# A decoder block on eight cores: sigmoids and the softmax division on ScalarE, another order for the output projection, and a prologue in 256-token pieces

## The reference, cut to what matters

```python
u = _rmsnorm(h, norm1_w[l])
proj = u @ w_in[l]                                    # (B,T,D_IN)
aq, ak, av, gq, gk, gv, g_lr, g_r, gate_a, gate_b = jnp.split(proj, offs, axis=-1)
attn_o = _swa_sink_attention(aq, ak, av, attn_sinks[l])   # window 128, softmax with one sink logit per head
gate_logit = (g_lr @ gla_gate_w2[l] + gla_gate_b[l]).astype(jnp.float32)
log_a = jax.nn.log_sigmoid(gate_logit) / GLA_GATE_NORMALIZER
gla_o = _gla(gq, gk, gv, log_a)                       # gated linear attention, 4 heads, state 256x512
gla_o = _rmsnorm(gla_o, gla_norm_w[l])                # per head
gla_o = gla_o * jax.nn.silu(g_r)
merged = jax.nn.sigmoid(gate_a) * attn_o + jax.nn.sigmoid(gate_b) * gla_o
h = h + merged @ w_out[l]
v2 = _rmsnorm(h, norm2_w[l])
h = h + (jax.nn.silu(v2 @ w_ffn_gate[l]) * (v2 @ w_ffn_up[l])) @ w_ffn_down[l]
return _rmsnorm(h, final_norm_w)
```

## Time and profile before

| | us |
|---|---|
| Three timed runs | 4012.56, 4039.02, 4191.10 (median 4039.02) |
| The profiled execution, its own time | 3989.18 |
| Its span, slowest core (core 5) | 3987.6 |
| Spans of all cores | 3979.7 to 3987.6 |
| Mean granted TensorE clock | 0.978 to 0.979 on all cores |
| TensorE busy (matmuls) | 3767.8 (94%) |
| VectorE busy | 1285.7 (32%) |
| ScalarE busy | 806.1 (20%) |
| Reciprocals on VectorE, 64 of 128x512 in the attention | 214.5 |
| ACT_TABLE_LOAD, 20 of them | 25.7 |

### The profile page before, as it was taken

One profiled execution on the slowest core, in us unless ns is written; L12 is line 12 of the kernel. 1 busy time (PEld: TensorE's weight loads), 2 busy tenths in 40 slices (PEclk: granted clock), 3 DMA queues, 4 the chain that ended last, 5 costly groups with the idle time before them and its releaser, 6 DMA issues.

```text
span 3987.6 us, 46220 instructions; the slowest of 8 cores (3979.7 to 3987.6 us)
## 1 busy us (share of the span) xinstructions
PE 3767.8 (94%) x18016; PEld 1700.6 (43%) x18016; DVE 1285.7 (32%) x2070; ACT 806.1 (20%) x1549; POOL 194.3 (5%) x361
## 2 busy tenths in 40 slices
PE   4899999996899999999999999999869999999998
PEld 1444444442344444444454444444324444444443
DVE  1225555556331110011112464646553111110113
ACT  1223232322221110000012232323313000000002
POOL 0000000000000000000000000000000000000000
PEclk9999999998999999999999999999989999999999
DMA  6234343435365555457863434333256555555553
GB/s 152 45 64 69 64 69 64 69 64 119 67 166 119 111 102 85 71 109 146 161 126 64 69 64 69 64 69 64 43 137 153 106 109 119 119 106 93 134 103 111
DMA packets 81416, 382.75 MB, mean 96 GB/s; under 512 B 9264, under 2 KB 10416, under 8 KB 44592
## 3 DMA queue, kind: packets, MB, share of 16 engines
q0 software_dynamic: 36432, 260.19, 39.2%
q1 hardware_dynamic: 44768, 119.59, 9.2%
HBM read 594.84 MB, written 44.04 MB: 160 GB/s over the span
## 4 chain that ended last, share of the span: by engine, by line
PE 91%; DVE 4%; DMA 2%; issue 1%; ACT 1%; POOL 0%; DVEq 0%; SPq 0%; ACTq 0%; POOLq 0%
PE ps L331 89%; DMA px_231<-xT 1%; DVE a_t_93 L378 1%; PE ps L339 1%; PE ps L619 1%; DMA h_0_96<-x 1%; DVE xnT_102 L375 1%; POOL st L399 0%; DVE xn_100 L375 0%; DVE mT L369 0%; ACT g_Sb L355 0%; DVE xn_101 L375 0%; DVE g_U L375 0%; DVE a_t_94 L364 0%; DVE a_t_93 L364 0%
## 5 line engine op out<-in xcount | busy, mean ns | idle before, releaser
L378 DVE RECIPROCAL a_t_93<-a_t_93 128x512 f32<-128x512 f32 x64 | 214.5, 3352 | 6.6
L355 ACT ACTIVATE sg_212<-ps 128x512 bf16<-128x512 f32 x88 | 52.5, 597 | 541.5 <-PE ps L331 541.5
L355 ACT ACTIVATE sg_213<-ps 128x512 bf16<-128x512 f32 x88 | 52.6, 598 | 527.8 <-PE ps L331 527.8
L331 PE MATMUL ps<-v2T_163,wu_67 128*128 128x512 bf16 x576 | 136.1, 379 | 0.0
L331 PE MATMUL ps<-v2T_108,wu_68 128*128 128x512 bf16 x576 | 136.1, 379 | 0.0
L331 PE MATMUL ps<-v2T_108,wu_65 128*128 128x512 bf16 x576 | 136.1, 379 | 0.0
L331 PE MATMUL ps<-v2T_108,wu_66 128*128 128x512 bf16 x576 | 136.1, 379 | 0.0
L331 PE MATMUL ps<-v2T_163,wu_69 128*128 128x512 bf16 x576 | 136.1, 379 | 0.0
L331 PE MATMUL ps<-v2T_108,wu_69 128*128 128x512 bf16 x576 | 136.1, 379 | 0.0
L331 PE MATMUL ps<-v2T_163,wu_66 128*128 128x512 bf16 x576 | 136.1, 379 | 0.0
L331 PE MATMUL ps<-v2T_163,wu_65 128*128 128x512 bf16 x576 | 136.1, 379 | 0.0
(11 more groups left out here) (1319 smaller groups left out, 6541.1 us busy)
## 6 DMA issues: line engine op xcount, KB each, us to landing
wu_66<-wmix POOLq DMA_DIRECT2D x24, 1024.0 KB, 13.1
wu_67<-wmix POOLq DMA_DIRECT2D x24, 1024.0 KB, 13.5
wu_65<-wmix POOLq DMA_DIRECT2D x23, 1024.0 KB, 14.4
wu_68<-wmix POOLq DMA_DIRECT2D x23, 1024.0 KB, 11.4
wu_69<-wmix POOLq DMA_DIRECT2D x22, 1024.0 KB, 14.1
wu_69<-wffn POOLq DMA_DIRECT2D x18, 1024.0 KB, 13.4
wu_65<-wffn POOLq DMA_DIRECT2D x18, 1024.0 KB, 14.1
wu_66<-wffn POOLq DMA_DIRECT2D x18, 1024.0 KB, 13.6
```

Of the source, the lines that this page charges most:

```text
L331: r = e.matmul(o_, lhsT=l_, rhs=r_, start=s0, stop=s1)
L355: S.op("act", lambda e: e.activation(out=o_, in_=i_, func=func, scale=scale, **kw), outs, ins)
L378: S.op("dve", lambda e: e.reciprocal(out=o_, in_=a), [o_], [a])
```

## The change

Five things are changed.

1. **Sigmoids.** The two token-major gates (g_r, gate_b) used one Tanh on ScalarE and one VectorE operation each. Now `sigm` makes three ScalarE operations (Exp, Ln, Exp), and VectorE does one product; the second sigmoid is written as bfloat16 (`ttb`). gate_a used Tanh and a VectorE operation; now ScalarE writes exp(-gate_a) straight to its place, and the rest of the sigmoid is part of the division below.
2. **Division.** In `a_back` the denominator is multiplied by 1 + exp(-gate_a) on VectorE, and its inverse is taken by Ln and Exp on ScalarE instead of by the VectorE reciprocal. The separate product with the gate falls away.
3. **End of a head.** `g_chain` yields once more, ahead of the last `s3`, and `weave` no longer runs the overlay to its end. What is left of it is put in front of the next overlay (`chain2`), which gets 18 steps instead of 16.
4. **Order of w_out.** `d_groups` goes through column groups 0 and 1 with the first four tiles, then with the last four, then through groups 2 and 3; one step of the attention rest follows each of the first tiles, where two did.
5. **Prologue.** x comes as four pieces of 256 tokens (`xq`, 2 MB in four transfers each), in twelve buffers. The pieces and the weights are issued on the POOL queue. A sixth weight buffer (printed as `wu_247`) exists for the first pass. Squares are added up on VectorE, so that the sum over inputs is four float32 matmuls per piece; Ln and Exp take the place of square root and reciprocal. The keys and values of the pieces, and the first head's values (`gv`), are computed between the norms. Most constants are set after the second piece.

```diff
+    wu.append(place("wu%d" % NW, [128, 8, 512], BF16, rE))
...
-    free_units = list(range(NW))
+    free_units = list(range(NW + 1))
...
-    def pump():
-        while free_units and wst["next"] < len(plan):
+    def pump(n=999):
+        while n > 0 and free_units and wst["next"] < len(plan):
+            n -= 1
             i = wst["next"]
             wst["next"] += 1
             u = free_units.pop(0)
             where[i] = u
             src, n = plan[i]
...
     def drop(units):
-        free_units.extend(units)
+        free_units.extend(u for u in units if u < NW)
         pump()
...
+    def first_norm_load(p):
+        for kg in range(4):
+            i = (p * 4 + kg) % 12
+            o_, src = px[i][:, :, :].rearrange("p a b -> p (a b)"), xq[p, kg]
+            S.op("pool", lambda e, o_=o_, src=src: e.dma_start(out=o_, in_=src), [o_], [], dma="px%d" % i)
+
+    def first_norm(p):
+        for kg in range(4):
+            sq = psq[kg % 2] if kg else pacc
+            act(sq[:], px[(p * 4 + kg) % 12][:], AF.Square)
+            if kg:
+                vtt(pacc[:], pacc[:], sq[:], ALU.add)
+        b = nps()
+        mm([(b[:, 0:256], onesf[:], pacc[:, q, :], q == 0, q == 3) for q in range(4)])
+        r = prs[p % 2]
+        act(r[:], b[:, 0:256], AF.Ln, scale=1.0 / D, bias=epst[:, 0:1])
+        act(r[:], r[:], AF.Exp, scale=-0.5)
         for k in range(16):
...
+            stt(xin[0][:, k, p * 256:(p + 1) * 256], px[(p * 4 + k // 4) % 12][:, k % 4, :], n1c[:, k:k + 1], r[:],
+                ALU.mult, ALU.mult)
...
+    def sigm(o_, t, p):
+
+        act(t, p, AF.Exp, scale=-1.0)
+        act(t, t, AF.Ln, bias=1.0)
+        act(o_, t, AF.Exp, scale=-1.0)
...
-            act(t[:], b[:, :], AF.Tanh, scale=0.5)
-            stt(rs[:, i, :], t[:], 1.0, b[:, :], ALU.add, ALU.mult)
+            sigm(t[:], t[:], b[:, :])
+            vtt(rs[:, i, :], t[:], b[:, :], ALU.mult)
...
-                act(t[:], b[:, :], AF.Tanh, scale=0.5)
-                vts(ag[:, pr, hf * 512:(hf + 1) * 512], t[:], 0.5, 0.5, ALU.mult, ALU.add)
+                act(ag[:, pr, hf * 512:(hf + 1) * 512], b[:, :], AF.Exp, scale=-1.0)
...
-        recip(t1[:], t1[:])
-        vtt(t2[:], bo[:, :], t1[:], ALU.mult)
-        vtt(v4(t3[:, :]), v4(t2[:, :]), ag[:, :, n * 128:(n + 1) * 128], ALU.mult)
+
+        stt(v4(t1[:, :]), ag[:, :, n * 128:(n + 1) * 128], 1.0, v4(t1[:, :]), ALU.add, ALU.mult)
+        act(t1[:], t1[:], AF.Ln)
+        act(t2[:], t1[:], AF.Exp, scale=-1.0)
+        vtt(t3[:], bo[:, :], t2[:], ALU.mult)
...
             store(sd[h], U[:, :, :].rearrange("p a b -> p (a b)"), "us", ("sd", h))
+        yield
         s3(NT - 1)
         yield
...
-        for _ in overlay:
-            pass
-
...
+        for g, ts in ((0, range(half)), (1, range(half)), (0, range(half, NT)), (1, range(half, NT)),
+                      (2, range(NT)), (3, range(NT))):
...
     first_norm_load(0)
-    pump()
+    pump(2)
+    S.op("pool", lambda e: e.dma_start(out=wg[:, :, :].rearrange("p a b -> p (a b)"), in_=wglr), [wg[:]], [], dma="c5")
+    first_norm_load(1)
+    pump(2)
+    first_norm_load(2)
...
             first_norm(0)
+            first_norm_load(3)
+            pump()
+            kv(0)
             first_norm(1)
+            kv(1)
+            constants()
+            gv(0)
+            gv(1)
+            first_norm(2)
+            gv(2)
+            gv(3)
+            kv(2)
+            first_norm(3)
+            gv(4)
+            gv(5)
+            kv(3)
+            drop(ukv)
+            gv(6)
+            gv(7)
+            drop(uv)
...
-                weave(g_proj(c, h), prev, 32, 16)
+                weave(g_proj(c, h), prev, 32, 18)
...
-                prev = a_chain(c, h, range(NT))
+                prev = chain2(ov, a_chain(c, h, range(NT)))
...
-        for i in range(8):
+        for i in range(12):
             next(dg)
             next(ac, None)
-            if i > 0:
-                next(ac, None)
```

More of the change, by code:

```diff
@@ L274, in build_nc @@
     tts = [G["tt0"], G["tt1"]]
+    ttb = [place("ttb%d" % i, [128, 512], BF16, S.base[tts[i].name][0]) for i in range(2)]
     e8, _ = seq(rE, [("a_P%d" % i, [128, 512], BF16) for i in range(4)] + [("a_t1", [128, 512], F32),
@@ new lines, in build_nc, with constants @@
+    vset(epst[:], EPS)
+    def constants():
+        stg = place("cstage", [128, 4, 128], F32, rXV[1] + 24576 + 4096)
+        load(stg[:], cst, "c1")
+        load(w2[:], w2r, "c4")
+        vcopy(identf[:], stg[:, 0, :])
+        vcopy(identb[:], stg[:, 0, :])
+        vcopy(trilb[:], stg[:, 1, :])
+        vcopy(amask[:], stg[:, 2:4, :])
+        vset(smask[:], 1.0)
+        vset(smask[:, :].rearrange("p (a b) -> p a b", b=128)[:, :, 0:1], 0.0)
+        vset(onesb[:], 1.0)
+        vset(mhalf[:], -0.5)
+        vset(declast[:], 0.0)
+        act(sinkc, sinkc, AF.Exp)
+        vts(negb, negb, -1.0, None, ALU.mult)
@@ L770, in d_groups @@
         h1 = h1lo + h1hi[c]
-        for g in range(4):
-            units = take(2)
-            for t in range(NT):
+        held = {}
+        half = NT // 2
+        for g, ts in ((0, range(half)), (1, range(half)), (0, range(half, NT)), (1, range(half, NT)),
+                      (2, range(NT)), (3, range(NT))):
+            if g not in held:
+                held[g] = take(2)
+            units = held[g]
+            for t in ts:
                 b = nps()
@@ L786, in d_groups @@
                 yield
-            drop(units)
+            if ts[-1] == NT - 1:
+                drop(units)
     def e_groups(c):
@@ L1064, in make_in_maps @@
     cst[:, 3] = j <= i
-    smk = np.ones((128, 512), np.float32)
-    smk[:, 0::128] = 0.0
     shared = {
```

118 lines of the change are left out of this document (50 added, 68 removed).

## The result

The changed kernel takes 3872.86 us (median; 4052.74 before), 0.958 of the kernel before with an interval of 0.946 to 0.970: faster. Its profiled execution took 3860.02 us against 3989.18, 129 us less where the sum had 141. In a second series the median was 3887.58 us, ratio 0.958 [0.952, 0.964].

What follows compares the result with a forecast made beforehand. TensorE, busy 3767.8 of 3987.6 us, was taken as the bound, leaving its stops and cold clock to win. 41 + 32 + 2 x (6 + 28) = 141 off 3989.18 gave 3848 profiled, 3884 timed; range 3830 to 3950.

Steps and rivals of the forecast that it cites:

- Prologue, 41: Start of kernel: first head's values end at 131 instead of 172.1 us, gain 41 us, bounds 22 to 46.
- pieces and weights in turn: Rival, prologue: alternating issue puts piece 1 at 30 and the values' end at 109, gain 63 us; under 1%.
- End of a head, 32: Heads 0 to 2, both chunks: six stops and the cold matmuls behind them vanish, gain 32 us.
- The wait on `g_gn_83` in the middle of a head stays: Middle of a head: TensorE's wait on this linear-attention buffer was claimed to remain, so no gain there.
- Head 3, 6 per chunk: Head 3: three stops per chunk, 1.2 us shorter each, and about 1.6 at the end; 6 us with the clock.
- Start of w_out, 28 per chunk: First w_out tiles beside attention blocks: nine tiles take 45 to 46 us instead of 75.3, gain taken as 28.
- Woven heads, nothing: Woven heads: TensorE stays busy 108 of 108 us, so sigmoids and division change nothing; ScalarE rises to 65.5.
- Table loads, 20 to 4, costing nothing: ScalarE's table loads shrink from 20 to about 4, but lie beside other work, so no gain.
- the prologue did bring something: Answers a rival, 14%: prologue brings nothing, pieces 1 to 3 standing behind 12 MB of weights; price 41 us, 3925.
- the division did not merely change its place: Answers a rival, 13%: VectorE waits for ScalarE's Exp, blocks in head 3 and w_out stay 12 us; 40 less, 3924.
- ScalarE did not become the bound: Answers a rival, 3%: ScalarE holds TensorE up in each of 48 blocks of the woven heads; +288 us, 4170.
- From the sum to the median: Whole kernel: from 3848 us in the profiled execution's terms to a timed median between 3871 and 3898, taken as 3884.

Runs made afterwards that it cites:

- e9_sums: Changed kernel with pieces and units in turn, constants copied late, and each piece's squares and sums issued one step earlier: clean cores 3803 to 3817 us.
- e1_turn: Changed kernel with pieces of x and weight units really in turn on POOL's queue: clean cores 3830 to 3845 us, ratio 0.952 to the kernel before.
- e8_const: As `e1_turn`, but constants are copied on VectorE only behind the last keys and values: clean cores 3823 to 3837 us, ratio 0.950 to the kernel before.
- e3_end: Changed kernel with the old end of a head, overlay drained and last tile's steps joined: 31 us more, ratio 0.977 to the kernel before.
- e4_tanh: Changed kernel with the sigmoids of g_r and gate_b by Tanh as before: clean cores 3855 to 3862 us, 4 to 9 more than the changed kernel.
- before_again: The kernel before, run again unchanged to see its clock by stretch: six cores show 0.81 from 340 us, none right behind the prologue.
- after_again: The changed kernel, run again unchanged to see its clock by stretch: six of eight cores show 0.81 behind the prologue.
- e2_turn_sp: As `e1_turn`, but pieces of x go down SP's queue beside the units on POOL's: clean cores 3847 to 3855 us, ratio 0.962 to the kernel before.

## Why the prediction was right, step by step

The time came within 12 us of the forecast, in the range and on its side. Most terms stand, one was left out, and two were too large. Part of the nearness is luck: the sum was 12 too high (141 against 129 in the profiles), and what was added for the timed median, 36, was 23 too much (12.8 measured), so that two errors worked against each other. In the second series the median lies 4 above the forecast.

- **Prologue, 41: too large, 30.2.** Piece 1 landed at 58.5, not 53, since a unit took 6.3 us and not the 5.8 chosen; and the stops before the sums of pieces 2 and 3 were 4.7 and 4.5 us, where 2.4 and 3.5 had been put down. The sums behind these stops ran at the low clock, 3.5 us each (92.80 to 96.34, 115.90 to 119.44) where 1.7 had been put down. `e9_sums` shows what these stops are: not the work of squares and sums, as the step had it, but their place in the in-order queues of ScalarE and VectorE, behind the evacuations of the piece before (the squares of piece 2 begin on ScalarE at 85.19, behind the copy of the first value group at 84.71); the run moves the place in both at once. The bounds of 22 to 46 held. That all six units stand ahead of piece 1 was read rightly from the order; `e1_turn` and `e8_const` show that it cost some 22 us at the values' end, together with the copy of the constants, while the 63 of the rival "pieces and weights in turn" left out what the constants then block, and the sums. What the parts of the 30 are worth each (pieces, fewer sums, the moved value projection, Ln and Exp) was not run apart.
- **End of a head, 32: right.** No wait is left at the end of heads 0 to 2; undone alone, 31 us.
- **"The wait on `g_gn_83` in the middle of a head stays": wrong.** It shrank from 2.6 to 1.5 us in chunk 0 and from 2.3 to between 1.5 and 1.75 in chunk 1, and behind the shorter stop the next matmuls stay warm (8 matmuls in 1.89 us, 2.27 before). Heads 0 to 2 gave 46.1 us in two chunks, of which `e3_end` explains 31. About 5 of the 15 left belong to the end of a head too, whose stop is 0.8 us shorter in `e3_end` than before (3.56 against 4.36; why stays open); the rest is this wait and the cold products behind it. Tanh, old end and reciprocal each leave the wait at 1.5, so it is none of these. What remains is the gate of attention: before, VectorE waited there for ScalarE's Tanh to scale it, with this head's products and state update queued behind; now the Exp goes straight into the buffer. That is read from the two timelines and by exclusion, and was not run alone. The rows below, VectorE before, show the waiting scale:

```profile
487.46 0.43 DVE L371 TENSOR_SCALAR a_g_105<-tt_79 128x512 bf16<-128x512 f32 x1 [1.60 <-ACT tt_79 L355]
...
489.52 1.40 DVE L375 SCALAR_TENSOR_TENSOR g_U<-g_U,dec,ps 128x512 f32<-128x512 f32 x2
```

- **Head 3, 6 per chunk: right**, 6.0 and 5.9, by stops of 3.3 us, 1.2 less than 4.5 as it said.
- **Start of w_out, 28 per chunk: too large, 20.** The step read 61.5 us for five tiles from a stretch that ended too late: the sixth tile had begun at 1026.99 (first row, kernel before), so five tiles took 55.4; the tenth began at 1042.88 (second row), so nine took 71.3 and not 75.3. And after, nine tiles took 51.2 (third row: the tenth begins at 962.31), not 46, at clock 0.88: the one stop that was expected with 2.2 us is 4.5 on five cores and 2.5 to 3.3 on the others, with cold products behind it, and another 1.1 us is a wait on `h_0`. 71.3 less 51.2 are the 20. So one of the step's own signs of being wrong did come: with two tiles in it, the first block took 14.4 us (917.29 to 931.69), more than the 13.2 before with one. "Bounds 14 to 38" held; that the order alone brings at least the four free tiles held too (15.6).

```profile
1026.99 3.59 PE L331 MATMUL ps<-wu_65,mT 128*128 128x512 bf16 x8
...
1042.88 1.89 PE L331 MATMUL ps<-wu_67,mT 128*128 128x512 bf16 x8
```

```profile
962.31 1.90 PE L337 MATMUL ps<-wu_69,mT 128*128 128x512 bf16 x8
```

- **Woven heads, nothing: right for the sigmoids** (`e4_tanh`) and for ScalarE's load, 58 us of 108 where 65 had been expected. For the division it is only half the truth: the new weave with the old reciprocal would have cost up to 2.9 us a head.
- **Table loads, 20 to 4, costing nothing:** they are 4, and 68 cost at most the 4 to 9 us of `e4_tanh`.
- **Rivals:** the prologue did bring something (30), the division did not merely change its place (7.8 per chunk in w_out), ScalarE did not become the bound.
- **From the sum to the median:** 36 us were put between the profiled execution and the timed median, as the kernel before had them, and 12.8 were measured. Lowered stretches fit both: in the timed execution of 3885.71 us the slowest core, 3884 us, has a mean clock of 0.978 where the clean ones have 0.984 to 0.988. That the 36 before were such stretches is inferred. The 23 too many more than made up for the 12 by which the sum promised too much.

## What to carry to other kernels

Before a queue is given a transfer "first", print what really stands ahead of it, and after each repair ask which instruction of an in-order engine waits next: here it was a copy of constants that nobody needed yet, then sums behind evacuations; with the place in the queue, these repairs were worth 41 to 43 us, more than the 30 of the first prologue change. Two stages of a chain that share a window of filler work are to be costed together, since the order decides what the shorter chain is worth. When a stretch is read off for a term, end it at an instruction, not at a round number.

## What the runs showed of the hardware

- A granted clock of 0.81, between the two levels of 1.2 and 2.4 GHz, is held in stretches on dense work: 303 matmuls in 80 us where a clean core runs 379. 76 of 82 such stretches in the kept traces last 160 to 163 us, wherever they begin: 340 to 502 within the heads (`before_again`), 924 to 1086 around w_out (`e1_turn`), 101 to 262 from the prologue on (`after_again`), the last with a TensorE stop of 4.5 us inside. So the end is not set by what the program does there. A stretch sits on a pair of cores and begins some microseconds behind a stop, when the clock had already come back to 1.00. The six exceptions are all in `after_again`: two of 18 us, two of 332 us, and two of 231 and 239 us that end with the kernel; what sets the length stays open. The Trainium skill, "TensorE: Matmul & The Clock Gate", section "Seeing it yourself", tells of a limiter that takes a whole die to 13/16 (0.8125) once three of its cores run dense matmuls, and holds it while the load lasts; the ratio agrees with the trace, but here cores of one die differ, and all eight run dense work at 1.00 for most of the span.
- Plain loads on SP and casting loads on POOL landed in turn, a tile of 512 KB for each unit of 1 MB (`e2_turn_sp`): 2 MB of x needed 26.8 us beside the weights, and 12.2 ahead of them in one queue. Which one was needed first made no difference.
- 256 KB on SP took 14.9 to 16.2 us beside units and pieces on POOL (`e1_turn`), and 2.8 in the changed kernel with nothing else under way.
